# L2 norms of q and k per token, carried by beta, the triangular matrix and the output rows

## The reference, cut to what matters

```
qkv = silu(causal_conv(concat(gq, gk, gv), conv_w))     # 3 x 512 channels
beta = sigmoid(gbeta)                                   # per token and head
q = q * rsqrt(sum(q*q) + eps) * 128**-0.5               # sum over the head's 128 channels
k = k * rsqrt(sum(k*k) + eps)
k_beta = k * beta
m = strict_lower(k_beta @ k.T) * decay                  # chunks of tokens
u, w = solve(I + m, [v * beta, k_beta * exp(g)])
o = (q * exp(g)) @ state + ((q @ k.T) * decay) @ (u - w @ state)
out = o * rsqrt(mean(o*o) + eps) * gain                 # per head, then gated
```

## Time and profile before

| | us |
|---|---|
| median of 3 runs (lowest, highest) | 2293.07 (2291.71, 2294.51) |
| the profiled execution | 2294.12 |
| its span in the profile | 2292.3 |
| PE busy, of the span | 2082.2 (91%) |
| DVE busy | 697.4 (30%) |
| ACT busy | 538.4 (23%) |

### The profile page before, as it was taken

How to read it: one execution, slowest core, us unless ns; L and a number is a source line. 1 busy time by engine, 2 the same in 40 slices (tenths; PEclk the granted TensorE clock), 3 DMA queues, 4 the chain that set the end, 5 groups by cost and what they waited for, 6 DMA issues and landing times.

```text
span 2292.3 us, 22349 instructions
## 1 busy us (share of the span) xinstructions
PE 2082.2 (91%) x9178; PEld 1262.6 (55%) x9178; DVE 697.4 (30%) x989; ACT 538.4 (23%) x818; POOL 110.1 (5%) x118
## 2 busy tenths in 40 slices
PE   6999969998999999989898978999999899999998
PEld 5766543333333333333332756788777678887866
DVE  4635130010101010101010667622667332224234
ACT  4224120000000000000000553233443233224134
POOL 3420000000000000000000000230000000000000
PEclk9999979999999999999998989998999999999998
DMA  9410619999999999999998221101123212223320
GB/s 233 145 65 2 255 75 403 427 427 428 428 429 429 428 429 429 428 429 429 428 428 357 109 101 55 56 19 37 56 73 129 74 49 98 101 82 129 111 92 37
DMA packets 46116, 512.28 MB, mean 223 GB/s; under 512 B 5585, under 2 KB 5713, under 8 KB 10593
## 3 DMA queue, kind: packets, MB, share of 16 engines
q1 hardware_dynamic: 43616, 504.72, 54.1%
q0 software_dynamic: 2432, 6.61, 1.3%
HBM read 507.08 MB, written 4.19 MB: 223 GB/s over the span
## 4 chain that ended last, share of the span: by engine, by line
PE 69%; DMA 21%; DVE 6%; ACT 3%; issue 1%; SPq 0%; POOL 0%; ACTq 0%; DVEq 0%
DMA arena<-in_w_gu_dram 19%; PE bank L2165 11%; PE bank L2187 5%; PE bank L855 4%; PE bank L854 4%; PE bank L856 4%; PE bank L538 3%; PE bank L539 3%; PE bank L540 3%; PE bank L1998 2%; PE bank L2122 2%; PE bank L879 2%; PE bank L881 2%; PE bank L880 2%; PE bank L2150 2%; PE bank L1858 1%
## 5 line engine op out<-in xcount | busy, mean ns | idle before, releaser
L2165 PE MATMUL bank<-arena 128*64 128x512 f32 x2048 | 485.7, 631 | 81.5 <-DMA arena<-in_w_gu_dram 80.8
L2165 PEld LDWEIGHTS bank<-arena 128*64 128x64 f32 x2048 | 163.4, 145 | 374.0 <-issue 373.0
L2568 DVE TENSOR_TENSOR arena<-arena,bank 128x256 f32<-128x256 f32 x64 | 27.0, 421 | 692.4 <-ACT arena L2774 692.4
L2187 PE MATMUL bank<-arena 128*64 128x512 f32 x1024 | 232.3, 594 | 0.7 <-ACT arena L2778 0.6
L2774 ACT ACTIVATE arena<-bank 128x256 f32<-128x256 f32 x64 | 24.6, 384 | 565.8 <-PE bank L2165 565.8
L2187 PEld LDWEIGHTS bank<-arena 128*64 128x64 f32 x1024 | 76.2, 137 | 141.3 <-issue 141.3
L854 PE MATMUL bank<-input_rounded,weight_rest 128*128 128x512 f32 x352 | 140.9, 400 | 4.9 <-DVE weight_rest L1276 4.9
L855 PE MATMUL bank<-input_rest,weight_rounded 128*128 128x512 f32 x352 | 141.0, 401 | 0.0
L856 PE MATMUL bank<-input_rounded,weight_rounded 128*128 128x512 f32 x352 | 138.9, 394 | 0.0
L538 PE MATMUL bank<-input_rounded,weight_rest 128*128 128x512 f32 x312 | 132.3, 424 | 4.8 <-DVE weight_rest L929 4.8
L539 PE MATMUL bank<-mix_rest,unit_rounded 128*128 128x512 f32 x312 | 126.9, 407 | 0.0
(11 more groups left out here) (460 smaller groups left out, 2932.0 us busy)
## 6 DMA issues: line engine op xcount, KB each, us to landing
arena<-in_w_gu_dram SPq DMA_DIRECT2D x128, 2048.0 KB, 28.7
arena<-in_w_d_dram SPq DMA_DIRECT2D x64, 2048.0 KB, 25.2
arena<-in_wpack_dram SPq DMA_DIRECT2D x83, 1024.0 KB, 4.9
arena<-in_x_dram SPq DMA_DIRECT2D x2, 2048.0 KB, 8.9
arena<-in_xT_dram SPq DMA_DIRECT2D x2, 1024.0 KB, 7.2
x_kept<-arena SPq DMA_DIRECT2D x4, 512.0 KB, 2.6
arena<-x_kept SPq DMA_DIRECT2D x1, 2048.0 KB, 7.9
out_dram<-arena SPq DMA_DIRECT2D x4, 512.0 KB, 2.6
```

The lines of the kernel that those rows point to most:

```text
L2165: last = mm(ab[64 * x:64 * x + 64, :], xsT[:, k, 64 * x:64 * x + 64], w[x][:, k, :], start=k == 0, stop=k == KD - 1)
L2187: last = mm(bank[4 + n][64 * x:64 * x + 64, :], hidT[c % 2][:, P * t + 64 * x:P * t + 64 * x + 64], w[:, x, t, 512 * n:512 * n + 512], sta ...
```

## The change

The square of a tile stays, but moves ahead: ACT makes it at steps u = 3 to 10 (three buffers in turn). TensorE sums per token instead: a block of 128 channels by 128 tokens of squares is the stationary operand and one column of ones moves, so that a tile takes four products with one column each, into `bank[4]` as 128 tokens by 32 (token tile, head). Their places in TensorE's list are behind tiles 5 to 11, and the last between the halves of the first value unit. Root, reciprocal and four products of beta and the factors are then made once, on 128x32 or 128x16. q and k keep their lengths. beta times 1/|k| scales v (`beta1`), times 1/|k| once more (`beta2`) it scales the triangular matrix's columns through L650 and the keys through `ebg`; 1/|q| times 128^-0.5 scales the output rows, which takes four ACT copies of 128x128 with a per-token scale at L1507 in place of one of 128x512.

```diff
             def l2_sum(t):
-                pe.wait_ge(S("l2_sq"), nth("l2_sq", t + 1))
-                if t >= 2:
-                    pe.wait_ge(S("l2_sd"), t - 1)
-                if t == 1:
-                    pe.wait_ge(S("gc_copied"), 1)
-                    pe.wait_ge(S("eg_made"), nth("eg_made", 1))
-                mm(l2bank[t % 2][:, :], ones, tmp(t % 2), start=True, stop=True).then_inc(S("l2_filled"), 1)
+                pe.wait_ge(S("l2_sq"), t + 1)
+                for n in range(NT):
+                    last = mm(bank[4][:, 8 * n + t:8 * n + t + 1], tmp(t % 3)[:, P * n:P * n + P], ones[:, 0:1], start=True, stop=True)
+                last.then_inc(S("l2_filled"), 1)
...
-                if u >= 8:
-                    l2_sum(u - 8)
-            for t in range(4, 8):
-                l2_sum(t)
-                value_half(t - 4, 0)
-                if t < 7:
-                    value_half(t - 4, 1)
-            value_half(3, 1)
+                if u >= 5:
+                    l2_sum(u - 5)
+            for v in range(4):
+                value_half(v, 0)
+                if v == 0:
+                    l2_sum(7)
+                value_half(v, 1)
...
-                    last = mm(hv(bank[1], h), beta[:, n, h:h + 1].to_broadcast([P, P]), ident, start=True, stop=True)
+                    last = mm(hv(bank[1], h), beta2[:, n, h:h + 1].to_broadcast([P, P]), ident, start=True, stop=True)
...
-            def l2_scale(t):
-                dve.wait_ge(S("l2_sd"), t + 1)
-                own(dve.reciprocal(tmp(2 + t % 2), tmp(2 + t % 2)))
-                own.wait()
-                stt(out=qkv[:, t, :], in0=qkv[:, t, :], scalar=DK ** -0.5 if t < 4 else 1.0, in1=tmp(2 + t % 2),
-                    op0=ALU.mult, op1=ALU.mult).then_inc(S("l2_done"), 1)
...
-            for t in range(3, 8):
-                l2_scale(t)
-                if t >= 5:
-                    rest_unit(U_MV + t - 5 + 2)
-            rest_unit(U_MV + 3 + 2)
+            dve.wait_ge(S("l2_filled"), nth("l2_filled", 8))
+            ts(l2, bank[4][:, 0:32], EPS, None, ALU.add).then_inc(S("l2_var"), 1)
+            rest_unit(U_MV + 2)
+            dve.wait_ge(S("l2_sd"), 1)
+            own(dve.reciprocal(l2, l2))
+            own.wait()
+            dve.wait_ge(S("beta_made"), nth("beta_made", 1))
+            own(tt(out=beta1, in0=beta, in1=l2h[:, :, 4:8], op=ALU.mult))
+            own(ts(l2h[:, :, 0:4], l2h[:, :, 0:4], DK ** -0.5, None, ALU.mult))
+            own.wait()
+            own(tt(out=beta2, in0=beta1, in1=l2h[:, :, 4:8], op=ALU.mult))
+            own.wait()
+            tt(out=ebg, in0=eg, in1=beta2, op=ALU.mult).then_inc(S("l2_done"), 1)
+            for v in range(3, 6):
+                rest_unit(U_MV + v)
...
             def l2_square(t):
-                if t >= 2:
-                    act.wait_ge(S("l2_filled"), nth("l2_filled", t - 1))
-                fn(tmp(t % 2), qkv[:, t, :], ACT.Square).then_inc(S("l2_sq"), 1)
+                act.wait_ge(S("cv_silu"), t + 1)
+                if t >= 3:
+                    act.wait_ge(S("l2_filled"), nth("l2_filled", t - 2))
+                fn(tmp(t % 3), qkv[:, t, :], ACT.Square).then_inc(S("l2_sq"), 1)
...
+                if 3 <= u < 11:
+                    l2_square(u - 3)
...
+            act.wait_ge(S("l2_var"), 1)
+            fn(l2, l2, ACT.Sqrt).then_inc(S("l2_sd"), 1)
+            for v in range(2, 6):
+                round_unit(U_MV + v)
...
-                fn(oa[:, n, :], bank[n % 2][:, :], ACT.Copy).then_inc(S("oa_made"), 1)
+                for h in range(4):
+                    last = fn(hv(oa[:, n, :], h), hv(bank[n % 2], h), ACT.Copy, scale=l2h[:, n, h:h + 1])
+                last.then_inc(S("oa_made"), 1)
```

More of the change, by code:

```diff
@@ L297, in program @@
         GS = B + 19472
+        l2 = view(GS, 32)
+        l2h = view(GS, NT, 8)
+        beta1 = view(GS + 32, NT, 4)
+        beta2 = view(GS + 48, NT, 4)
         gate = view(GS + 128, NT, 16)
@@ L386, in program @@
         mvbank = [bank[5], bank[7], bank[0], bank[1]]
-        l2bank = [bank[4], bank[6]]
         hhi = [rounded(f"input_rounded{k}", 4096 + 512 * k, L) for k in range(KD)]
@@ L590, in aside @@
                     elif v == 0:
-                        pe.wait_ge(S("l2_sd"), 8)
+                        pe.wait_ge(S("gc_copied"), 1)
+                        pe.wait_ge(S("eg_made"), nth("eg_made", 1))
                     else:
@@ L624, in second_pe @@
                         .then_inc(S("gc_filled"), 1)
-                if u >= 8:
-                    l2_sum(u - 8)
-            for t in range(4, 8):
-                l2_sum(t)
-                value_half(t - 4, 0)
-                if t < 7:
-                    value_half(t - 4, 1)
-            value_half(3, 1)
+                if u >= 5:
[5 more added lines that the diff above has]
+                value_half(v, 1)
             aside(0)
             aside(1)
-            pe.wait_ge(S("l2_done"), nth("l2_done", 8))
-            pe.wait_ge(S("beta_made"), nth("beta_made", 1))
+            pe.wait_ge(S("l2_done"), 1)
             for n in range(4):
@@ L1006, in second_dve @@
                     dve.tensor_copy(gc.rearrange("p n h -> p (n h)"), bank[6][:, 64:80]).then_inc(S("gc_copied"), 1)
[L1007 to L1010, removed]
-            for t in range(3, 8):
-                l2_scale(t)
-                if t >= 5:
-                    rest_unit(U_MV + t - 5 + 2)
-            rest_unit(U_MV + 3 + 2)
-            dve.wait_ge(S("l2_done"), nth("l2_done", 8))
+            dve.wait_ge(S("l2_filled"), nth("l2_filled", 8))
[13 more added lines that the diff above has]
+                rest_unit(U_MV + v)
+            dve.wait_ge(S("l2_done"), 1)
             def aside_scale(v):
@@ L1076, in second_dve @@
                 own(tt(out=h3(kdc[:, n, :]), in0=h3(bank[4][:, :]), in1=per_token(edec, n), op=ALU.mult))
-                own(tt(out=h3(vbt[:, n, :]), in0=h3(bank[5][:, :]), in1=per_token(beta, n), op=ALU.mult))
+                own(tt(out=h3(vbt[:, n, :]), in0=h3(bank[5][:, :]), in1=per_token(beta1, n), op=ALU.mult))
                 own.wait()
```

## The result

| | before | after |
|---|---|---|
| median of 20 runs each, us | 2294.8 (2291.55 to 2298.54) | 2277.19 (2274.08 to 2301.79) |
| the profiled execution's span | 2292.3 | 2274.0 |
| DVE busy | 697.4 | 666.1 |

The ratio is 0.993, 95% interval 0.9919 to 0.9942: 13 to 19 us faster. The forecast was 2276, the range 2271 to 2282. One run of the changed kernel took 2301.79 us at a mean granted clock of 0.91; its other 19 end at 2283.86 and have 0.956 to 0.961.

The account below looks back on a forecast made before the run. The prediction took TensorE's list, with its stalls around the norms, to bound the kernel. Stalls -14.0, half clock -3.15, sums -1.5 and delayed gates +1.4 made -17.2 us: forecast 2276 us, range 2271 to 2282.

Parts of the forecast that it names:

- What bounds: Whole kernel: TensorE holds 69% of the chain, DVE 6%; DVE time counts only where TensorE stands still for it.
- (a): TensorE stalls before sum 0, sum 4, value unit 2 and aside unit 17 go: together 14.0 us gained.
- (b): Half clock (1.2 GHz) of TensorE behind those stalls goes with them: 3.15 us gained.
- (c): Sums on TensorE behind L623: eight old at 0.86 us become six paying new at 0.90, gain 1.5 us.
- (d): Sum 0 and square 2 added ahead of L623: gates come 1.4 us later; stall stays, about 5.8 us.
- (e): Output rows on ACT: four scaled copies cost 0.54 us more, four times, covered by idle time; at most 2.2 us.
- (f): DVE loses eight times 3.35 + 0.69 us, ACT eight roots: worth nothing beyond the stalls that go.
- Sum: Whole change: -14.0 - 3.15 - 1.5 + 1.4 = -17.2 us, forecast 2276 us.
- Rival 1: At `l2_var` or a rounding, one stall over 4 us with half clock stays: 6 us, 2282; chance 0.10.
- rival 3: Narrow sums cost TensorE's clock: small form 10.5 us, 2286.5, chance 0.03; large form 49 us, 2325, chance 0.03.
- rival 4: Preparation bound by something of fixed time, so an earlier L648 only waits: no change, 2293; chance 0.02.
- rival 2: Sums at half price give 2.7 us, or shorter half clock behind L623 up to 1.2: 2272; chance 0.08.

Follow-up runs that it names:

- e1: Changed kernel with eight unused 128x512 reciprocals put back on VectorE where the old ones stood: 2286.82 us, ratio 0.9964.
- e6: Kernel before with a reciprocal of 16 tokens instead of 512, whose values scale all tokens (wrong norms): 2282.18 us, ratio 0.9944.
- e7: Kernel before with its first two squares one step earlier on ScalarE: 2287.77 us, ratio 0.9965.
- e9: Kernel before with both the 16-token reciprocal (wrong norms) and the first two squares a step earlier: 2276.6 us, ratio 0.992.
- e4: Changed kernel with every one-column product issued twice into the same column: 2279.87 us, ratio 0.9936.
- e11: Changed kernel with sum 2 ahead of the gates' wait (L624) instead of behind it, second run of that kernel: 2272.72 us, ratio 0.9906.
- e5: Changed kernel with one unscaled 128x512 copy per output tile in place of four scaled 128x128 ones: 2276.21 us, ratio 0.9915.

## Why the prediction was right

- **What bounds.** TensorE's list, with the stalls around the norms: right. e1 brings one of them back by DVE time alone, larger than before; e6 and e7 take them out of the old kernel, one cause each, and e9 both, all but 1.9 us.
- **(a) and (b), stalls and their half clock, 14.0 + 3.15 us.** None of the four is left. With the five sums they make the third stretch, -19.74 us against -19.5. Of the two causes e6 shows the reciprocals' (9.3 us of stage), e7 the first square's (4.5). The slack of about 3 us ahead of value unit 2 was 2.9.
- **(c), the size of a sum.** 0.90 us forecast, and doubling shows 0.89 on the path. The row of the first block was the right one. The Trainium skill ("TensorE: Matmul & The Clock Gate", section "Wait — 56ns, not 53.3ns?") has about 62 ns for each small matmul where the hardware's own decoding is off. With a new stationary operand for each, e4 shows 0.89 / 8 = 111 ns, so a sum priced by that figure alone, which counts no load of the operand, comes out too cheap.
- **(d), what comes ahead of the gates.** +1.41 us for +1.4; the stall 5.83 for 5.8. Right, though so close a hit took some luck: from the anchor to the gates' sum the profiles of e1 and e11 need 1.5 us more than the 63.12 of the changed kernel, in half clock behind the stall at L620. But sum 2 behind L624 was counted at 0.90 and the stretch grew by 1.84. It is the one term mis-sized: the half clock was taken as fixed, while it lost 3.75 us instead of 2.8. In the same list it lost 2.6 to 3.8.
- **(e), the four copies.** Covered: idle 1.72 for 2.27, e5 within the spread.
- **(f)** DVE's 31 us less of busy time were worth nothing beyond the stalls: e9 keeps the eight roots, scalings and wide sums, with short reciprocals, and has the same time.
- **Sum.** -17.2 forecast, -16.5 in the stage; the spans differ by 18.3, of which 0.5 us lie behind the stage and 1.3 ahead of it, where nothing was changed; the medians differ by 17.6. The forecast of 2276 started from the median of 3 runs, 2293.07; from that of 20, 2294.8, the same sum gives 2277.6. Rival 1 (a stall left), rival 3 in both forms and rival 4 didn't come; of rival 2 the cheaper sum didn't, and the half clock behind L623 moved the other way. The row that spoke for rival 3 comes and goes from profile to profile with the same list.

## What to carry to other kernels

An engine at 30% can hold one at 91%: read what stands in its list ahead of the small operation for which the busy engine waits, here weight rests behind 3.35 us reciprocals. A reciprocal on data repeated over the partitions costs by its columns (3.35 us for 512, 0.35 for 32, 0.25 for 16), so make it per token, where it is once 0.35 us. The sums' form earned its gain through that short reciprocal and through places for the squares and sums; e9, with the old form and a reciprocal of 16 tokens that gives wrong norms, reached the same time. Part of it was to be had for less: moving two squares one step earlier (e7) gave 7 us and leaves the values as they are. After such a change look at the stalls that remain: moving one small sum behind one more unit took another 9.9 us from the stage.

## What was not expected of the hardware

TensorE's half clock behind a stall is not a fixed price. Behind the gates' stall the same list lost 2.6 to 3.8 us. Behind a stall of 1.61 us, equal in two kernels, the granted clock was 0.69 over the next 6.45 us in one and 1.00 in the other. Behind the stall of 1.69 us at L620 it was 1.00 for 6.1 us in the changed kernel and 0.78 for 7.6 us in e1 and e11, a loss of 1.5 us. Wide passes that follow 16 narrow ones in the first block, with no idle time between, were slowed by 1.2 GHz in five of thirteen profiles and ran at 2.4 GHz in eight. In e4 such differences gave back 2.9 us behind the stage; so a change of a few microseconds has to be read in the profile's stage and not from the total, and better from more than one profile.
